# A hybrid decoder step on one core: the last gathered row added on TensorE, the first loads in order of arrival, and the first modulation blocks laid out by the host

## The reference, cut to what matters

```python
mod = silu(c) @ w_ada[l] + b_ada[l]              # 1024 x 6144, c: one row for the prompt, 8 for the samples
sh1, sc1, g1, sh2, sc2, g2 = split(mod, 6)
h = rmsnorm(x, norm1_g[l]) * (1 + sc1) + sh1
proj = h @ w_in[l]
mix = concat(pool_mix(proj), attention(proj), state_space(proj))
x = x + g1 * (mix @ w_out[l])
h2 = rmsnorm(x, norm2_g[l]) * (1 + sc2) + sh2
idx = top 8 of 64 experts, gates w
x = x + g2 * (sum_k w[k] * expert[idx[k]](h2) + shared(h2))
...
y = rmsnorm(x, final_g)                          # after the last layer
```

## Time and profile before

| | |
|---|---|
| three executions | 1657.77, 1664.03, 1666.68 us, median 1664.03 |
| the profiled execution | 1663.45 us, its span 1661.8 us, mean granted clock of TensorE 0.966 of 2.4 GHz |
| PE busy | 1551.2 us, 93% of the span |
| DVE, POOL, ACT busy | 960.6, 499.3, 239.7 us |
| DMA | 567.06 MB at a mean of 341 GB/s |
| chain that ended last | PE 83%, DVE 11%, issue 2%, DMA 2%, SP's queue 1%, ACT 1% |

### The profile page before, as it was taken

How to read it: one execution, slowest core, us unless ns; L and a number is a source line. 1 busy time by engine, 2 the same in 40 slices (tenths; PEclk the granted TensorE clock), 3 DMA queues, 4 the chain that set the end, 5 groups by cost and what they waited for, 6 DMA issues and landing times.

```text
span 1661.8 us, 30299 instructions
## 1 busy us (share of the span) xinstructions
PE 1551.2 (93%) x11197; PEld 1006.3 (61%) x11197; DVE 960.6 (58%) x2476; ACT 239.7 (14%) x607; POOL 499.3 (30%) x562
## 2 busy tenths in 40 slices
PE   7898999999999999999789989899999999999994
PEld 4675676555566556666467648655555566666663
DVE  3787547655555645544479673775555554454456
ACT  3233431000002100000031332310000000000001
POOL 1304203433433333332102150043333333333310
PEclk9999899999999999999889979999999999999996
DMA  9568386999999999999875684789999999999963
GB/s 340 215 252 313 112 339 254 391 402 419 418 416 412 398 417 407 406 389 368 326 270 202 240 284 158 313 313 406 413 417 417 413 409 412 398 395 407 400 249 139
DMA packets 129366, 567.06 MB, mean 341 GB/s; under 512 B 30876, under 2 KB 47826, under 8 KB 94403
## 3 DMA queue, kind: packets, MB, share of 16 engines
q1 hardware_dynamic: 89490, 507.12, 77.3%
q0 software_dynamic: 39584, 57.61, 9.7%
q10 hardware_dynamic: 144, 0.40, 0.1%
HBM read 775.37 MB, written 56.95 MB: 501 GB/s over the span
## 4 chain that ended last, share of the span: by engine, by line
PE 83%; DVE 11%; issue 2%; DMA 2%; ACT 1%; SPq 1%; DVEq 0%; ACTq 0%; POOLq 0%
PE ps L1385 39%; PE ps L1398 19%; PE ps L1087 5%; PE ps L1233 4%; PE ps L1406 2%; PE ps L918 2%; PE ps L974 2%; PE ps L982 1%; PE ps L951 1%; DVE xTs L2205 1%; DMA yrows_k<-ytok,idx_y 1%; PE ps L947 1%; DVE scratch L2169 1%; PE ps L1165 1%; PE ps L1218 1%
## 5 line engine op out<-in xcount | busy, mean ns | idle before, releaser
L1385 PE MATMUL ps<-raw,xTs 128*64 128x256 f32 x4928 | 564.0, 381 | 9.8 <-DMA raw<-in_exp_w_gate_up 8.8
L1385 PEld LDWEIGHTS ps<-raw,xTs 128*64 128x64 f32 x4928 | 380.3, 138 | 140.7 <-issue 12.6
L889 POOL DMA_INDIRECT yrows_k<-ytok,idx_y x192 | 195.0, 1016 | 651.4 <-DVE ytok L2070 614.2
L2205 DVE STREAM_TRANSPOSE xTs<-xg 64x256 f32<-64x256 f32 x768 | 335.7, 437 | 12.0 <-DMA xg<-hrows,idx_x 4.3
L1398 PE MATMUL ps<-dn,scratch 128*64 128x512 f32 x1280 | 304.8, 594 | 23.5 <-issue 21.9
L2070 DVE COPY ytok<-ps 128x512 f32<-128x512 f32 x192 | 132.7, 691 | 230.0 <-PE ps L1398 229.8
L882 POOL DMA_INDIRECT xg<-hrows,idx_x x192 | 199.1, 1037 | 107.2 <-issue 57.2
L2064 DVE TENSOR_TENSOR scratch<-scratch,ps 128x128 f32<-128x128 f32 x192 | 55.2, 288 | 264.5 <-ACT scratch L1684 264.2
L1684 ACT ACTIVATE scratch<-ps 128x128 f32<-128x128 f32 x192 | 53.3, 278 | 1014.7 <-PE ps L1385 1014.7
L1398 PEld LDWEIGHTS ps<-dn,scratch 128*64 128x64 f32 x1280 | 97.3, 137 | 138.9 <-issue 121.2
L1385 PE MATMUL ps<-wide,xTs 128*64 128x256 f32 x1216 | 138.3, 379 | 0.0
(11 more groups left out here) (410 smaller groups left out, 1326.5 us busy)
## 6 DMA issues: line engine op xcount, KB each, us to landing
raw<-in_exp_w_gate_up SPq DMA_DIRECT2D x154, 2048.0 KB, 24.1
dn<-in_exp_w_down SPq DMA_DIRECT2D x160, 1024.0 KB, 23.7
wide<-in_exp_w_gate_up SPq DMA_DIRECT2D x38, 2048.0 KB, 24.6
narrow<-in_exp_w_down SPq DMA_DIRECT2D x32, 1024.0 KB, 22.1
wide<-in_w_ada SPq DMA_DIRECT2D x20, 1024.0 KB, 9.5
narrow<-in_w_ada SPq DMA_DIRECT2D x18, 1024.0 KB, 8.7
wide<-in_w_in SPq DMA_DIRECT2D x16, 1024.0 KB, 7.5
ypart<-yrows_k SPq DMA_DIRECT2D x16, 1024.0 KB, 7.0
```

The source lines that it names most:

```text
L889: pool.indirect_dma_start(yrows_k.rearrange("t (h d) -> (t h) d", h=2), bass.IndirectOffsetOnAxis(ap=idx_y[:, b:b + 1], axis=0), ytok[n % ...
L1385: ins = mm(ps[64 * h:64 * h + 64, 2 + n % 2, 0:256], xTs[n % 2][:, k, :, :].rearrange("p u i -> p (u i)"), w[:, k, h], start=k == 0, stop= ...
L2205: ins = v.transpose(xTs[n % 2][64 * e:64 * e + 64, :, u, :], xg[n % NX][64 * u:64 * u + 64, 256 * e:256 * e + 256].rearrange("p (k j) -> p ...
```

## The change

The host lays the first four modulation blocks of each layer out as `ada_first`, one row of 16 KB for each partition, and a block is one DMA of 128 such rows in place of two DMAs of 512 runs of 2 KB. The start waits for its loads by three semaphores in the order in which they are needed, the conditioning first, and block 0 is multiplied ahead of the bias table and of the squares. At the end of a layer choice 6 is loaded as soon as step 94 is scattered. `ysum` goes through PE as a plain matmul with the identity, and choice 7, the last row, is multiplied on PE with a diagonal matrix of its gates (`ydiag`) and added in PSUM, so that DVE adds seven choices and not eight. After layer 1 ACT does a `Sqrt` of one column ahead of the squares.

```diff
-PARTS_AFTER = [NSTEP - TOPK + 2 * g + 1 for g in range(TOPK // 2)]
+PARTS_AFTER = [min(NSTEP - TOPK + 2 * g + 1, NSTEP - 2) for g in range(TOPK // 2)]
...
         def early_ada(layer, q):
-            for j in range(2):
-                sp.dma_start(half_block(early_at(layer, q)[:, j]), block_columns(a["w_ada"][layer], q, j)).then_inc(ada_loaded[q].sem, 16)
+            sp.dma_start(early_at(layer, q)[:, :, :].rearrange("p j n -> p (j n)"), a["ada_first"][layer, q]).then_inc(ada_loaded[q].sem, 16)
...
-        load(start_loaded, cst[:, :], a["consts"])
+        load(cond_loaded, xrows[0:1, 3, :], a["c_prompt"])
+        load(cond_loaded, xrows[1:NC, 3, :], a["c_sample"])
+        load(cond_loaded, cst[:, :], a["consts"])
         for t in range(2):
-            load(start_loaded, xrows[:, t, :], a["x_prompt"][0, P * t:P * t + P, :])
...
+            load(x_loaded, xrows[:, t, :], a["x_prompt"][0, P * t:P * t + P, :])
+        load(x_loaded, xrows[0:NS, 2, :], a["x_sample"][:, 0, :])
+        early_ada(0, 0)
+        load(rel_loaded, relb[:, :], a["rel_bias"])
+        load(rel_loaded, poolrow[0:KD, 0:P], a["final_g"].rearrange("(k p) -> k p", p=P))
+        for q in range(1, ADA_FIRST):
             early_ada(0, q)
...
             parts(2)
+            parts(3)
             scattered(NSTEP - 1)
             sp.dma_start(ysam[:, :], yrows_k[TOPK * NP_:TOPK * T, :]).then_inc(ysam_loaded.sem, 16)
-            parts(3)
+            for t in range(2):
+                sp.dma_start(ypart[t][3][:, 1, :], ytok_k[P * t:P * t + P, TOPK - 1, :]).then_inc(y_last_loaded[t].sem, 16)
...
+            W(y_loaded[3][0], 16)
+            warm(7, 6)
+            for t in range(2):
+                W(y_summed, t + 1)
+                for c in range(KD):
+                    mm(ps[:, c, P * t:P * t + P], ysum[t][:, P * c:P * c + P], ident, start=t == 0, stop=False, skip_group_check=True)
             W(ysam_loaded, 16)
             W(gsel_ready)
             for c in range(KD):
-                ins = mm(ps[:, c, NP_:T], ysam[:, P * c:P * c + P], gsel[:, :], start=True, stop=True, skip_group_check=True)
+                ins = mm(ps[:, KD - 1, NP_ + NS * c:NP_ + NS * c + NS], ysam[:, P * c:P * c + P], gsel[:, :],
+                         start=False, stop=True, skip_group_check=True)
             ins.then_inc(sam_made.sem, 1)
-            W(sam_added)
-            W(y_loaded[3][0], 16)
-            warm(7, 6)
-            W(y_summed, 1)
+            W(ydiag_ready)
+            W(y_last_loaded[0], 16)
             for c in range(KD):
-                turn(ps[:, c, 0:P], ysum[0][:, P * c:P * c + P], P)
-            W(y_summed, 2)
+                if c == KD - 1:
+                    W(sam_added)
+                mm(ps[:, c, 0:P], ypart[0][3][:, 1, P * c:P * c + P], ydiag[0], start=False, stop=True, skip_group_check=True)
+            W(y_last_loaded[1], 16)
             for c in range(KD):
-                turn(ps[:, c, P:2 * P], ysum[1][:, P * c:P * c + P], P).then_inc(moe_turned.sem, 1)
+                mm(ps[:, c, P:2 * P], ypart[1][3][:, 1, P * c:P * c + P], ydiag[1],
+                   start=False, stop=True, skip_group_check=True).then_inc(moe_turned.sem, 1)
                 if c >= 3:
                     sum_square(0, squares_1, layer + 1, c - 3, sumsq.sem)
...
         prepare_exp(0)
+        ada_copy(0, 0, 0)
+        for h in range(HEADS):
+            se.wait_ge(start_ready, KD + h + 2)
+            act_(skews[:, h, 0:PAST + 1], ps[:, 4 + h, 0:PAST + 1], ACT.Copy).then_inc(start_copied_a, 1)
         prepare_more(0)
         prepare_sin(0)
+        ada_copy(0, 1, 1)
         se.wait_ge(sumsq.sem, sumsq.by(0, 1))
         root(3)
...
+            else:
+                act_(sm[:, 20:21], epsilon, ACT.Sqrt)
             square(x_part, squares_1, layer + 1)
```

More of the change, by code:

```diff
@@ L380, in program @@
     ysam = placed("ysam", "rowsP", 0, [NS * TOPK, D], F32)
+    ydiag = [scratch[:, 2592 + P * t:2592 + P * t + P] for t in range(2)]
+    assert PICK + 768 + 1024 <= 2592 and 2592 + 2 * P <= 3072
     ypart_at = [("kbuf", 0), ("kbuf", SEG), ("narrow", 0), ("mixT", 0), ("narrow", SEG), ("hT", 0), ("vbuf", 0), ("vbuf", SEG)]
@@ L423, in program @@
     sines_ready = sig("sines_ready", 1 + SC // 2)
-    ada_loaded = [sig(f"ada_loaded{q}", 32) for q in range(ADA_FIRST)]
+    ada_loaded = [sig(f"ada_loaded{q}", 16) for q in range(ADA_FIRST)]
     x_part = sig("x_part", KD)
@@ L506, in program @@
     y_loaded = [[sig(f"y_loaded{g}_{t}", 16) for t in range(2)] for g in range(4)]
+    y_last_loaded = [sig(f"y_last_loaded{t}", 16) for t in range(2)]
     ysam_loaded = sig("ysam_loaded", 16)
@@ L921, in times_one @@
             return mm(dst, src, ident[0:n, 0:n], start=True, stop=True)
-        pe.wait_ge(start_loaded, 16 * 8)
+        pe.wait_ge(cond_loaded, 16 * 3)
+        pe.wait_ge(start_silu, 1)
+        for k in range(KD):
+            ins = turn(ps[:, 4, NC * k:NC * k + NC], xrows[0:NC, 3, P * k:P * k + P], NC)
+        ins.then_inc(start_ready, 1)
+        pe.wait_ge(x_loaded, 16 * 3)
         for k in range(KD):
@@ L1457, in _ @@
         chain = Links(se, alink)
+        se.wait_ge(cond_loaded, 16 * 3)
+        act_(xrows[0:NC, 3, :], xrows[0:NC, 3, :], ACT.Silu).then_inc(start_silu, 1)
         early_parameters(se, 0)
[L1459 to L1463 removed]
         quarter, epsilon = sm[:, 0:1], sm[:, 1:2]
@@ L1862, in angles @@
             ts(a0, a0, -3.1415925, 3.1415925, ALU.max, ALU.min).then_inc(angle_ready.sem, 1)
-        prepare_first(0)
-        prepare_angle(0)
+        chain(v.memset(condT[:, :, :], 0.0))
+        dve.wait_ge(start_ready, 1)
+        cp(condT[:, :, 0:NC], ps[:, 4, 0:KD * NC].rearrange("p (a b) -> p a b", a=KD)).then_inc(start_vector, 1)
+        for k in range(KD):
+            dve.wait_ge(start_ready, k + 2)
+            cp(xT[:, k, :], ps[:, k % 4, 0:T]).then_inc(x_part.sem, 1)
+        prepare_first(0)
+        dve.wait_ge(rel_loaded, 16 * 2)
+        cp(relbw[:, :, :], relb[:, :].unsqueeze(2).to_broadcast([32, HEADS, P]))
+        for m in range(2):
+            ins = cp(relbs[:, :, :, m], relb[:, :].unsqueeze(1).to_broadcast([32, NS, HEADS]))
+        ins.then_inc(start_vector, 1)
+        prepare_angle(0)
+        dve.wait_ge(start_ready, KD + HEADS + 2)
+        dve.wait_ge(start_copied_a, HEADS)
+        cp(finalg[:, :], ps[:, 1, 0:KD])
+        chain(cp(biasS[:, :], ps[0:ROWS, 2, 0:PAST + 1]))
+        dve.sem_inc(x_ready.sem, 1)
+        dve.sem_inc(start_vector, 1)
         norm_root(0, 1)
@@ L2268, in _ @@
                     gates(n - 2)
+                elif n == 5:
+                    W(gk_ready)
+                    for t in range(2):
+                        ins = ts(ydiag[t], ident, gk[:, t, TOPK - 1:TOPK], None, ALU.mult)
+                    ins.then_inc(ydiag_ready.sem, 1)
                 if layer + 1 < DEPTH and n == PREP_STEP + 1:
```

109 lines of the change are left out of this document (45 added, 64 removed).

## The result

| | before | after |
|---|---|---|
| median | 1663.42 us (20 executions, 1657.77 to 1666.68) | 1664.93 us (20 executions, 1663.51 to 1673.24) |
| ratio | | 1.0025, 95% interval 1.0016 to 1.0034 |
| profiled execution | 1663.45 us, span 1661.8 | 1665.02 us, span 1663.3 |
| PE busy | 1551.2 us | 1556.4 us |
| DMA packets | 129366 | 122646, the same 567 MB |

I had predicted 1652.0 (1647 to 1661). The time did not fall; it is 0.25% longer, less than the 0.5% that I called the limit of telling, but its interval does not include 1. The range did not hold it.

The account below looks back on a forecast made before the run. PE carries 83% of the chain, with a stall near step 91 caused by SP's issue. Terms -11.6 - 1.5 + 1.8 - 0.2 = -11.5 against the profiled 1663.45 give 1651.95, said as 1652 us, range 1647 to 1661.

Parts of the forecast that it names:

- The stall: Near step 91 of layer 0, PE waits on SP's long block 1 issue; removing it gains 0 to 11.56 us, whole taken.
- whether the traffic fits: Check on the stall's gain: from 777 to 790 us 5 MB must move, and 13 us at 391 GB/s just fit 5.1 MB.
- The reading of 147 GB/s: While SP was held, queues moved 147 GB/s against 417 when full, so memory's rate did not hold the issue.
- Half of the stall moves: Rival: near step 91 PE waits for data instead of SP, half of 11.56 us left, 1658 us; chance 0.15.
- SP is held all the same: Rival: queued bytes, not the number of runs, hold SP near step 91, so 11.56 us return, 1664 us; chance 0.13.
- the sum by the rule of the Trainium skill: If 2 KB runs lose nothing against 16 KB, the block layout is worth 0 and the time is about 1664 us.
- Slower than before: Rival: the clock stays at 1.2 GHz at both ends of a layer, 15.4 us more, 1670 us; chance 0.04.
- Start: Kernel's beginning, reordered loads and block 0 ahead of table and squares: -2.1 or +2.0 us depending on clock, taken as -1.5.
- End of layer 0: PE's sequence behind the modulation grows from 10.3 to 12.7 us, +2.4 (at most +10.1); with 0.6 us of faster transfers, +1.8.
- End of layer 1: Same 12.7 us sequence with PE starting earlier, +0.3, less 0.5 for the table load: -0.2 us, range -2 to +8.

Follow-up runs that it names:

- ten_before: Kernel before, with the filled rows of block b beginning at place 10b modulo 64 instead of place 0; 1631.72 us, ratio 0.9813.
- ten_after: The whole change, with the filled rows of block b beginning at place 10b modulo 64; 1633.71 us, ratio 0.9820 to the kernel before.
- start_tail: The changed kernel with the old layout of the modulation blocks (two DMAs of 512 runs of 2 KB); 1666.23 us, ratio 1.0025 to the kernel before.
- tail_only: Kernel before with the new end of a layer alone, old layout and old start; 1666.41 us, ratio 1.0018.
- layout_only: Kernel before with the 16 KB layout of the modulation blocks and nothing else; 1660.42 us, ratio 0.9981.
- ten_layout: Kernel before with the 16 KB block layout and filled rows beginning at place 10b modulo 64; 1629.16 us, ratio 0.9800.
- the rows spread: Filled rows spread evenly over a block's 64 places, in four kernels; on the kernel before 1674.24 us, ratio 1.0074.
- with 10.0: Filled rows of block b beginning at place 10b modulo 64, in several kernels; on the kernel before 1631.72 us, ratio 0.9813.
- with 4.0: Filled rows of block b beginning at place 4b modulo 64, in four kernels; on the kernel before 1635.14 us, ratio 0.9834.

## Why the prediction was wrong

**The stall: the event right, its worth wrong.** SP's issue, the conditional load and steps 92 and 93 came as written. The step that failed is the sentence "What is late next is nothing on SP, because the loads behind (the parts and blocks 2 and 3) are each released by a step of PE and move forward with it", and with it the choice to "take the whole" of 0 to 11.56. Their *issues* move forward with PE: part 1 goes at 803.88 and not 816.24, block 3 at 808.74 and not 821.09. Their *landings* do not. I had asked whether the traffic fits and looked at 777 to 790. The stretch to ask about was 790 to 835, where three parts and two blocks, 10.5 MB, are behind one another, 25 us at 417 GB/s. In both kernels that stretch ends near 835. Of the 11.6 us, 3.2 were left with the layout alone, and none that can be told with the whole change.

**The reading of 147 GB/s.** I took the slow stretch of the earlier trace rows for proof that the queues were nearly empty. It was an average over 16 engines, most of them done and a few still behind: eleven shares of the expert's load above had landed by 776.8, the last at 789.9. With 5.39 us a step the experts ask for 3.15 MB in 8.09 us, 389 GB/s, and for 17.3 MB of gathers and scatters in some 545, 32 more: by this estimate 421 in sum, where a full stretch moves 417. From 280 to 760 us 405 GB/s were moved in the kernel before and 413 in `ten_before`, both with a DMA share of 1.00 or 1.01. A stage that asks for all the queues can give is bound by the busiest of them, and such queues have little left for a PE that is 11.6 us ahead.

**The rivals.** "Half of the stall moves" had the right mechanism ("PE no longer waits for SP but for data: a down load or block 2 behind the burst") at half its size: it left 5.8 us, and 3.2 were there. "SP is held all the same" had nearly the right time, 1664, by a mechanism that did not occur; so did the sum by the rule of the Trainium skill (DMA: Bandwidth & Descriptors, Specifications) that runs from 512 B on reach the line rate, about 1664. As to rate the layout does show a little (the full stretch from 798 to 825 us moves 418 GB/s after, that from 807 to 834 393 before), and as to SP's time in the issue, 0.34 against 9 to 12 us, much. The small loss of the result is not the rival "Slower than before" either: the 32 matmuls with `ysum` took 3.73 us, 0.12 each, so the clock was not low behind the unread ones.

**Start.** In the profiled execution it came as worked out, at the good end: tokens' turns at 9.11 (9.0), squares ended at 26.6 (26.9), `prepare_mid` at 32.81, 2.27 us earlier. But it is one of two outcomes. The profile after, and then that of `ten_after`, whose start is the same code:

```profile
16.60 3.64 PE L973 MATMUL ps<-raw,condT 128*32 128x512 f32 x16
20.17 2.12 PE L1020 MATMUL ps<-cst,mixT 32*128 32x257 f32 x8
22.80 3.83 PE L950 MATMUL ps<-hT,cst 128*128 128x264 f32 x16
```

```profile
16.57 3.64 PE L973 MATMUL ps<-raw,condT 128*32 128x512 f32 x16
20.14 3.79 PE L1020 MATMUL ps<-cst,mixT 32*128 32x257 f32 x8
...
24.92 5.70 PE L950 MATMUL ps<-hT,cst 128*128 128x264 f32 x16
```

The clock rises within the table in the one and in the squares in the other (the durations tell it; the granted clock of this stretch reads 1.00 in both). I had seen both ends, -2.1 and +2.0, and taken the good one. Over nine profiles with the new start the first projection begins at 45.53 to 49.52, on average 47.54; over eleven with the old one at 47.05 to 48.92, on average 47.84. And by the first expert step the new start is behind, 274.75 (271.57 to 279.23) against 272.66 (271.15 to 274.96) on average. So the term was not -1.5 but about +2, and the step that failed in it is the choice between the two ends. What takes the time between the first projection and the experts stays open. The granted clock alone does not tell it: from 150 to 170 us it is 0.59 in the profile after, 0.71 in that of `ten_after` and 0.72 before, and the first expert steps there begin at 271.57, 276.63 and 272.85.

**End of layer 0.** +2.4 predicted for TensorE's sequence, and 2.7 in the profile up to the first square (3.2 up to the first projection, since each of the last columns is now two instructions and not one); alone it costs 3.0 (1.2 to 5 by its interval). Right, if a little low.

**End of layer 1.** -0.2 predicted, and 0.4 less than the 1.9 us that it was behind at the last down product. The table load is out of the way at 1618.00. Right.

In sum: -3.2 for the layout, +2 for the start, +3 for the end, +1.8 where +4.2 us (2.7 to 5.7) were measured. Start and end together, `start_tail`, measure +4.2 by themselves, so what is missing is the layout's 3.2, which the whole change does not show. Why it shows alone and not there is open, and so is why 7 of the 20 executions of the changed kernel took 1669.9 to 1673.2 us and the others 1663.5 to 1667.1. The 4 us between the outcomes of the start do not explain it alone: `tail_only`, with the old start, has two of 12 executions over 1669 us as well, `start_tail`, with the old layout, two of 7, and `layout_only` none of 11.

## What to carry to other kernels

A stall that lets full queues drain is no loss that can be taken back: before you count it as a gain, follow each load behind it to its landing, and compare the bytes a second that the stage asks for with what the queues give. Look at DMA engines one by one: a DMA share well below 1 while someone waits for a load, or a row of 1 us waits that no releaser explains, meant here that a few engines were behind. The best version here, `ten_layout`, is 2.0% faster than the kernel before by four short DVE operations in place of one and by leaving out the rest of this change but the layout.

## What the hardware showed that I had not expected

Which rows a gather or scatter leaves empty decides how many DMA engines fall behind: four and a fifth between with the places as before, eight with the rows spread. A gather or scatter here moves a block's 64 rows as 128 half rows, one to a partition. I had supposed neighbouring pairs of rows to go round the 16 engines, and the time with 10.0 came out as that gave (1631 to 1633), but the count of lagging engines fits another rule better. The Trainium skill (DMA: Bandwidth & Descriptors, The descriptor swizzle) gives for a plain transfer of 128 partitions four neighbouring partitions and the four 32 further to each engine. No trace here tells which engine moved what, so I worked out the shares: with the routing of these inputs in layer 0 that rule puts so many half rows on each engine, the gathers and scatters together (an estimate by that page's rule):

```
places as before   903 887 864 796 679 540 454 355 565 549 512 428 325 244 194 153
spread             889 243 871 233 854 220 845 205 859 225 829 211 802 196 783 183
turned by 4        494 513 530 514 515 512 512 534 538 563 590 590 553 504 496 490
turned by 10       537 533 534 537 526 531 517 527 531 527 530 531 546 521 503 517
```

Four heavy ones and a fifth between, eight heavy ones, three or four slightly heavy, none: the shares of a load lag in these numbers in the first three sets of runs (with 4.0 the last four come 1 to 9 us behind the twelfth). With 10.0 none stands out, but the shares of a load still land evenly over 9 us, which these numbers do not give. The rule does not explain why spreading, with the same maximum, cost 10 us more; its half-filled pairs may (826 packets of 2052 bytes from 280 to 760 us, 114 before), which was not tried. How these numbers turn into the 13.7 us that layer 1's experts lost, less than the excess of the heavy engines (375 rows at 0.08 us, 30 us), is open too.

SP's issue of two DMAs of 512 runs at that place took 8.86 to 12.49 us, that of one DMA of 128 runs with the same bytes 0.34 in every kernel. A hold of the issuing engine was no sign that time was being lost.
